# Gate and up projections of 16 experts in Strassen's scheme on 32-column tiles (fp32, one core)

## The reference

```python
cap = EC_CAPACITY_FACTOR * T // N_EXPERTS            # 128 prompt rows, 32 sample rows
aff = jax.nn.softmax((xt @ w_router).astype(F32), axis=-1)
g, idx = lax.top_k(aff.T, cap)
xe = xt[idx]
he = jax.nn.silu(jnp.einsum('ecd,edf->ecf', xe, w_gate)) * jnp.einsum('ecd,edf->ecf', xe, w_up)
ye = jnp.einsum('ecf,efd->ecd', he, w_down) * g[..., None].astype(h.dtype)
y = jnp.zeros((T, D), h.dtype).at[idx.reshape(-1)].add(ye.reshape(-1, D))
```

## Time and profile before

| | |
|---|---|
| Median of 3 runs | 2678.43 us (2675.58 to 2678.94) |
| Profiled execution | 2674.68 us, span 2672.6 us |
| TensorE busy | 2567.5 us, 96% |
| DVE / ACT / POOL busy | 42% / 18% / 12% |
| Granted TensorE clock, mean | 0.985 |
| Expert part | from about 1823 us to the end |

### The profile page before, as it was taken

One profiled execution on the slowest core, in us unless ns is written; L12 is line 12 of the kernel. 1 busy time (PEld: TensorE's weight loads), 2 busy tenths in 40 slices (PEclk: granted clock), 3 DMA queues, 4 the chain that ended last, 5 costly groups with the idle time before them and its releaser, 6 DMA issues.

```text
span 2672.6 us, 37000 instructions
## 1 busy us (share of the span) xinstructions
PE 2567.5 (96%) x15287; PEld 1810.1 (68%) x15287; DVE 1119.8 (42%) x2013; ACT 489.7 (18%) x1114; POOL 313.2 (12%) x310
## 2 busy tenths in 40 slices
PE   7999899999989999999999999977999999999997
PEld 4554455765667777774466477436899889889886
DVE  5556825266774121133430134374334333433433
ACT  3120000144451111102211022210111111111112
POOL 0120103200000101041210001100110010011001
PEclk9999999999999999999999999997999999999999
DMA  4110202000001001022101300236787778778776
GB/s 160 32 51 0 93 28 59 1 1 16 1 25 47 24 24 48 24 88 86 48 16 52 105 32 1 88 132 242 263 275 270 271 262 287 258 260 275 259 270 252
DMA packets 189947, 315.90 MB, mean 118 GB/s; under 512 B 6122, under 2 KB 69951, under 8 KB 189216
## 3 DMA queue, kind: packets, MB, share of 16 engines
q1 hardware_dynamic: 181952, 292.87, 31.6%
q0 software_dynamic: 7904, 21.76, 3.2%
HBM read 288.40 MB, written 26.21 MB: 118 GB/s over the span
## 4 chain that ended last, share of the span: by engine, by line
PE 90%; DVE 8%; ACT 1%; issue 1%; DMA 0%; SPq 0%; POOL 0%; POOLq 0%; DVEq 0%; ACTq 0%
PE banks L827 46%; PE banks L1158 9%; PE banks L1580 9%; PE banks L1018 5%; PE banks L1331 5%; PE banks L1247 5%; PE banks L1425 3%; PE banks L1038 3%; PE banks L1094 2%; DVE arena L2204 2%; PE banks L843 1%; PE banks L1053 1%; PE banks L1547 1%; DVE arena L2650 1%; DVE arena L2653 0%
## 5 line engine op out<-in xcount | busy, mean ns | idle before, releaser
L827 PE MATMUL banks<-arena 128*128 128x160 f32 (+3 forms) x7030 | 1332.6, 351 | 22.3 <-ACT arena L1691 8.0
L827 PEld LDWEIGHTS banks<-arena 128*128 128x128 f32 x7030 | 1050.8, 191 | 322.1 <-issue 268.6
L682 POOL TENSOR_TENSOR arena<-arena 128x512 f32<-128x512 f32 (+2 forms) x112 | 170.0, 1530 | 1208.8 <-DMA arena<-in_w_br_hyena 566.6
L1158 PE MATMUL banks<-arena 128*128 128x320 f32 x896 | 243.2, 432 | 0.5 <-ACT arena L1803 0.5
L1580 PE MATMUL banks<-arena 128*32 128x256 f32 x4320 | 236.2, 379 | 0.0
L1158 PEld LDWEIGHTS banks<-arena 128*128 128x128 f32 x896 | 169.8, 190 | 70.4 <-ACT arena L1803 1.0
L1580 PEld LDWEIGHTS banks<-arena 128*32 128x32 f32 x4320 | 138.9, 110 | 92.7 <-issue 2.5
L2735 DVE TENSOR_TENSOR arena<-arena,banks 128x160 f32<-128x160 f32 x128 | 41.1, 321 | 356.2 <-ACT arena L1956 324.1
L2745 DVE TENSOR_TENSOR arena<-arena 128x512 f32<-128x512 f32 x240 | 149.4, 684 | 14.3 <-DMA arena<-in_w_exp_down 14.3
L1018 PE MATMUL banks<-arena 128*128 128x512 f32 (+1 forms) x384 | 142.9, 522 | 2.5 <-DVE arena L2244 2.5
L1956 ACT ACTIVATE arena<-banks 128x160 f32<-128x160 f32 x120 | 36.5, 304 | 503.8 <-PE banks L827 503.8
(11 more groups left out here) (269 smaller groups left out, 1851.0 us busy)
## 6 DMA issues: line engine op xcount, KB each, us to landing
arena<-in_w_exp_gate SPq DMA_DIRECT2D x32, 2048.0 KB, 8.2
arena<-in_w_exp_up SPq DMA_DIRECT2D x32, 2048.0 KB, 13.1
arena<-in_w_exp_down SPq DMA_DIRECT2D x32, 2048.0 KB, 17.8
arena<-in_w_in SPq DMA_DIRECT2D x36, 512.0 KB, 4.4
arena<-in_x_prompt SPq DMA_DIRECT2D x8, 1024.0 KB, 8.5
residual_rows<-arena SPq DMA_DIRECT2D x10, 512.0 KB, 2.6
normed_rows<-arena SPq DMA_DIRECT2D x10, 512.0 KB, 2.6
arena<-residual_rows SPq DMA_DIRECT2D x5, 1024.0 KB, 13.6
```

The source lines that it names most:

```text
L682: done.inc(pool.tensor_tensor(out, l, r, op))
L827: last = pe.matmul(out, l, r, start=(n == 0), stop=(n == len(pairs) - 1))
L1158: last = pe.matmul(PS[:, 3 * (g % 2) + bank, 0:GN], l[:, k, :], r[:, k, :], start=(k == 0 and which in (G1, G2, G5)), stop=(k == 3), skip_ ...
```

## The change

Gate and up get the scheme that the down product has. The hidden width is cut in two halves h = 0 and 1. For each, the pair of matrices is (gate half, up half), both 1024x512, as if they were the left and right column halves of one matrix of 1024x1024; the third pair is that of down. So an expert has three stages with 9 units each. Names of sums in a stage: c11a and c11b (gate, first 64 slots on one side), c22a and c22b and c12a and c12b (up), c21a and c21b (gate, second slots), sg and sh (sample gate and hidden), ha and hb (the product silu(gate) times up for 256 columns). The order of units is MID or LATE: in LATE (second half, in the loop) the sample's unit s comes last.

Since slots are now stationary, the hidden values come with slots on partitions (`HR`, `HRQ`) and are turned back into `HE`: `turn_half` (4 transposes) twice, `turn_quarters` (2) once. ACT copies them out of PSUM. ACT also does the scaled slot copies into `XET` that DVE did (16 a pass). The weight sums are 8 for each stage on 1024 elements a partition: two `own_weights` for the stage itself (into `W4`), six `next_weights` for the next stage. The token sums of `XET` for the next expert are POOL's (`token_sums`). For expert 0, POOL makes the first six sums of the first pair as twelve of 128x512, before it gathers. The final rows are loaded after the first half of expert 15, into buffers of its first pair, and most of their squares come after its hidden values. Cut to its core:

```diff
+        MID = ("p1a", "p1b", "p6a", "p6b", "p7a", "p7b", "s", "p4a", "p4b")
+        LATE = ("p1a", "p1b", "p6a", "p6b", "p7a", "p7b", "p4a", "p4b", "s")
 # SP
+            def expert_pairs(e, first, which):
...
+                    if not first and n < 2:
+                        sp.wait_ge(sem["gu_mm"], GU * e + (9 * n - 9))
+                    if not first and n == 2:
+                        sp.wait_ge(sem["dn_mm"], e * DN)
...
+            sp.wait_ge(sem["gu_mm"], GU * (NE - 1) + 9)
             for i in range(NT // 2):
                 sp.dma_start(at(FIN_AT[i], 2, D), acc[2 * i * P:2 * (i + 1) * P, :]...
 # POOL
+            pool.wait_ge(sem["w_in_0"], 32)
+            for out, l, r in ((W1[0], b12, b11), (W2[0], b22, W1[0]), (b12, b12, b22)):
+                mixes.wait()
+                for k in range(4):
+                    half_sum(mixes, out[:, k, :], l[:, k, :], r[:, k, :], ALU.subtract)
...
             with pool.Fori(1, NE - 1) as e:
                 gather(e + 1, False)
+                token_sums(e + 1)
                 scatter(e, False)
 # TensorE
-            def gate_up(e, first):
-                wait("xet_ready", e * 4 + 4)
-                for f in range(FF // P):
...
+            def gate_up(e, h, first, order):
...
+                        elif name == "p4a":
+                            if h == 0:
+                                wait("x_sum", 5 * e + 5)
+                            wait("wt_sum", w_summed(e, h, 2))
+                            wait("gu_sum", summed(e, h, order, "c22a"))
+                            unit("gu_mm", (6, False, a22, W4, a_cols), (3, False, XS4, b22, a_cols))
...
+                unit("gu_mm", (7, True, a11, b11, b_cols), (7, True, a12, b21, b_cols))
+                if h == 1:
+                    wait("gu_sum", summed(e, 0, MID, "hb"))
+                    turn_half(0)
...
+            def expert(e, first):
+                gate_up(e, 0, first, MID)
+                gate_up(e, 1, first, LATE)
+                wait("gu_sum", summed(e, 1, LATE, "hb"))
+                turn_half(1)
+                turn_slots(e + 1, False)
+                down(e)
 # turn_slots: the quarter blocks use bank 1, in which the turned half lay
+                if not first:
+                    wait("he_ready", e * 4 - 2)
 # ACT
+                snapshot(e, 1, LATE, 5, "p7b")
+                second_silu(e, 1, LATE, 0)
+                second_silu(e, 1, LATE, 1)
+                snapshot(e, 1, LATE, 6, "s")
+                half_turned(e, 1, 2)
+                sample_silu(e, 1, LATE)
+                slot_blocks(e + 1, 0)
+                rows_down(e, first)
 # DVE
+            def weight_sum(out, l, r, k):
+                ks = slice(2 * k, 2 * k + 2)
+                dve.tensor_tensor(out[:, ks, :], l[:, ks, :], r[:, ks, :], ALU.subtract).then_inc(sem["wt_sum"], 1)
...
+            def second_half(e):
+                gate_first(e, 1, LATE, 0)
+                own_weights(e, 1, 0)
+                gate_first(e, 1, LATE, 1)
+                own_weights(e, 1, 1)
+                next_weights(e, 1, 1, 0)
+                next_weights(e, 1, 1, 1)
+                next_weights(e, 1, 2, 0)
+                up_second(e, 1, LATE, 0)
+                next_weights(e, 1, 2, 1)
+                up_second(e, 1, LATE, 1)
+                next_weights(e, 1, 3, 0)
+                up_first(e, 1, LATE, 0)
+                rows_hidden(e, 1, LATE, 0)
+                next_weights(e, 1, 3, 1)
+                up_first(e, 1, LATE, 1)
+                rows_hidden(e, 1, LATE, 1)
+                sample_gate(e, 1, LATE)
+                sample_hidden(e, 1, LATE)
```

More of the change, by code:

```diff
@@ L1542, in turn_slots @@
                 wait("gather_s", e * 16 + 16)
+                for half, bank in ((0, 0), (1, 2)):
+                    for k in range(4 * half, 4 * half + 4):
+                        last = pe.transpose(PS[:, bank, (k % 4) * P:(k % 4 + 1) * P], XE[:, tiles[k]], ident[:, :])
+                    last.then_inc(sem["xe_tr"], 1)
                 if not first:
[L1544 to L1548, removed]
+                    wait("he_ready", e * 4 - 2)
@@ L1549, in turn_slots @@
                 for c in range(2):
-                    last = pe.transpose(PS[:, 5, c * P:(c + 1) * P], XEQ[:, tiles[c]], ident[:, :])
+                    last = pe.transpose(PS[:, 1, c * P:(c + 1) * P], XEQ[:, tiles[c]], ident[:, :])
                 last.then_inc(sem["xe_tr"], 1)
-            def gate_up(e, first):
-                wait("xet_ready", e * 4 + 4)
-                for f in range(FF // P):
[L1556 to L1564, removed]
@@ new lines, in second_half_begun, with rows_down, copied @@
+            def second_half_begun(e, order):
+                snapshot(e, 1, order, 0, "p1a")
+                first_silu(e, 1, order, 0)
+                snapshot(e, 1, order, 1, "p1b")
+                half_turned(e, 0, 1)
+                first_silu(e, 1, order, 1)
+                snapshot(e, 1, order, 2, "p6a")
+                snapshot(e, 1, order, 3, "p6b")
+                snapshot(e, 1, order, 4, "p7a")
+            def rows_down(e, first):
+                def copied(n, name):
+                    rows, side = (upper, lower) if n < 6 else (lower, upper)
+                    gate = gnow[upper, 2:3] if n == 6 else gnow[lower, 0:1] if n >= 4 else gnow[lower, 1:2]
+                    act.wait_ge(sem["dn_mm"], e * DN + (MID.index(name) + 1))
+                    act.activation(KEPT7[n][rows, :], PS[side, 6 + (n % 2 if n < 6 else 0), 0:256], ACT.Copy, scale=gate
+                                   ).then_inc(sem["dn_kept"], 1)
@@ new lines, in added, with gate_first, up_second @@
+            def added(e, h, order, name, dst, src, n, rows):
+                dve.wait_ge(sem["gu_kept"], kept(e, h, n + 1))
+                dve.tensor_tensor(dst, src, KEPT7[n][rows, :], ALU.add).then_inc(sem["gu_sum"], 1)
+            def gate_first(e, h, order, n):
+                dve.wait_ge(sem["gu_mm"], unit_done(e, h, order, ("p1a", "p1b")[n]))
+                added(e, h, order, "c11", GP[upper, n, :], PS[upper, 6 + n, 0:256], n, upper)
+            def up_second(e, h, order, n):
+                added(e, h, order, "c22", UP[lower, n, :], PS[upper, 3 + n, 0:256], 4 + n, upper)
@@ L2766, in results @@
-            def results(e, first):
-                lower, upper = slice(0, CP // 2), slice(CP // 2, CP)
-                def added(dst, bank, rows, gate, n):
-                    dve.wait_ge(sem["dn_kept"], e * DKEPTS + (n + 1))
-                    dve.scalar_tensor_tensor(dst, PS[rows, bank, 0:256], gate, DKEPT[n][rows, :], ALU.mult, ALU.add
-                                             ).then_inc(sem["y_out"], 1)
+                for n, col in enumerate((gates[:, 0, bass.ds(e, 1)], gswap[:, bass.ds(e, 1)], gates[:, 1, bass.ds(e, 1)])):
+                    dve.tensor_copy(gnow[:, n:n + 1], col).then_inc(sem["gates_now"], 1)
```

528 lines of the change are left out of this document (365 added, 163 removed).

## The result

The changed kernel is slower. It takes 2786.62 us (median of four runs, 2784.56 to 2789.08); the kernel before, on the same chip, takes 2678.68 (four runs, 2675.58 to 2682.19). The ratio is 1.041, with a 95% interval of 1.039 to 1.042. The forecast was 2653.6, with a range to 2675: wrong in sign and by 133 us.

What follows compares the result with a forecast made beforehand. TensorE's own work was taken as the bound. Passes -28.6, expert 0 +0.7, selection +0.5 and end +2.6 made -24.8 from 2674.7: 2649.9, plus 3.7 for the median: 2653.6 us, range 2643 to 2675.

Steps and rivals of the forecast that it cites:

- TensorE's own work: TensorE in the loop: 27 units of 1.727 us plus turnings and changes make 49.3, pass 49.7 instead of 51.74.
- the chain without cover: End of the second half: last product, turnings and ACT's emptying of bank 1 leave TensorE waiting 0.3 to 0.5 us a pass.
- Whether DVE keeps up: DVE in the loop: 24 weight sums of 1.15 us and the rest make 39.8 of 49.7; adds ready when TensorE wants them.
- Rival (a): DVE becomes the bound, from 1.33 us a weight sum; 2711 us at 1.5. Chances 0.09 past 1.42, 0.08 between 1.33 and 1.42.
- (b): Lost cover adds up: flag restarts of 0.1 to 0.2 us and POOL's sums give pass 51.0, 2672 us; chance 0.10.
- POOL's token sums: Five POOL operations a pass during down: 3.4 us, DVE losing up to that, mostly covered by room; taken as 0.
- Before the experts and in expert 0: POOL's twelve first-pair sums, 16 us, beside DVE's selection: +0.5 us; second pair's late load in expert 0: +0.7 us.
- rival (c): POOL's twelve sums push the selection before the experts by 5 to 16 us: 2658 to 2669 us; chance 0.10.
- After the experts: Last expert: seven squares follow ACT's copy, delaying the root; DVE's chain ends at 57.9 us against 55.2, taken as +2.6.
- What the change takes from TensorE: Gate and up in the loop: 128 products, 34.8 us, become 18 units of 1.727, 31.1 us: 3.7 less a pass.
- What it adds on TensorE: Per pass: turning hidden values back 1.2 us, changes between kinds of product 0.3, and an uncovered wait of 0.3 to 0.5.
- Rival (d): Products on 32-column tiles don't keep their pitch, or the granted clock falls; slower; chance 0.02.

Runs made afterwards that it cites:

- written-out: The changed kernel with TensorE's loop over experts 1 to 14 written out as straight code, nothing else: 2652.61 us, ratio 0.991 to the kernel before.
- hinted one: The changed kernel with `hint_back_edge` on TensorE's loop, adding one branch prefetch instruction to the body, head not moved: 2656.47 us, ratio 0.992 to the kernel before.
- split root: The changed kernel with TensorE's loop written out and the final rows' root, reciprocals and scalings done in two parts of five tiles: 2646.86 us, ratio 0.989.
- aligned kernel: The changed kernel with the head of TensorE's loop moved to the start of a block of 256 instructions: 2712.33 us, ratio 1.013 to the kernel before.
- kernel before with the long body: The kernel before with two experts instead of one in the body of TensorE's loop, 7 passes and 6 jumps back: 2700.40 us, ratio 1.009.

## Why the prediction was wrong

**TensorE's own work.** Right. The pass was forecast at 49.7 and is 49.8 wherever no jump disturbs it: the first pass of the changed kernel and all passes of the written-out and the hinted one. In part that is luck, since two small misses cancel in it: 544 MATMULs in 29.56 are 17 units of 1.739, not 1.727, which makes 0.3 more for 27 units, and the chain without cover, put in at 0.3 to 0.5, costs nothing in the loop (below).

**Whether DVE keeps up.** Right. A weight sum's median in the written-out kernel is 1.226 us, and four in a row start 1.13 apart (W was 1.15). DVE is busy for 43.3 of 49.8 in a pass, 87%, where near 85% was forecast. The weight sums of the written-out kernel (min/median/max ns, first and last start), and then TensorE's waits in its experts on what DVE makes:
```profile
L2964 DVE TENSOR_TENSOR arena<-arena x370: 1206/1226/1752, 1833.8 to 2600.4; 128x1024 f32<-128x1024 f32 x185
```
```profile
PE banks L1631 <- DVE arena L2943: 1.9, 1, 1.9
PE banks L1631 <- DVE arena L2990: 1.2, 1, 1.2
PE banks L1614 <- DVE arena L3007: 1.2, 2, 0.7
```
All are single or double events in experts 0 and 15; none returns in each pass, so c22a, c22b and y were there when wanted. Rival (a) is out, and so is (b): the pass is not 51.0, and the turnings' wait, for which 0.3 to 0.5 a pass was put in, is 1.2 in all.

**POOL's token sums.** Too small: 3.4 forecast, 5.6 measured. POOL and DVE in time in the written-out kernel, with the idle time that precedes:
```profile
2072.21 1.03 POOL L811 TENSOR_TENSOR arena<-arena 128x256 f32<-128x256 f32 x1 [27.44 <-ACT arena L2124]
2073.32 0.73 POOL L813 TENSOR_TENSOR arena<-arena 128x256 f32<-128x256 f32 x1
2074.01 0.73 POOL L814 TENSOR_TENSOR arena<-arena 128x256 f32<-128x256 f32 x1
2074.70 1.44 POOL L815 TENSOR_TENSOR arena<-arena 128x128 f32<-128x128 f32 x1
2076.10 1.71 POOL L817 TENSOR_TENSOR arena<-arena 128x256 f32<-128x256 f32 x1
```
```profile
2074.16 3.06 DVE L2964 TENSOR_TENSOR arena<-arena 128x1024 f32<-128x1024 f32 x2 [0.74 <-PE banks L1631]
```
POOL's sum of 128 elements beside DVE takes 1.44, longer than one of 256 (0.73), and DVE's two sums take 3.06 where two cost 2.4. Each delays the other, as the sum of the earlier trace rows had shown. The step's figure was too small by 2.2 us, but what it put down as room did hide it: TensorE waits for none of it in the pass.

**Before the experts and in expert 0.** Right. The selection's wait grew from 12.97 to 13.5, the 0.5 forecast, and rival (c) did not come about. POOL's twelve sums took 15.4 us (16 forecast), from 1770.79 in the changed kernel, and DVE's MAX8 beside them took 0.68, as the mean of the kernel before (678 ns): no measurable slowing, nor of FIND_INDEX8 and MATCH_REPLACE8. Expert 0, from its first turning (1824.95) to the first product of expert 1 (1883.5), takes 58.6 in the written-out kernel against 57.9, for a forecast of +0.7.

**After the experts.** Right: in the written-out kernel the last expert starts at 2580.4 and DVE's chain ends at 2638.3, 57.9 later, the forecast number. The split root shows that the stated cause is the right one.

**The sum** with its four terms gave 2653.6; the written-out kernel, which does the same work, takes 2652.61. That they agree so closely is partly luck. The sum added 3.7 us for the distance of the median from the profiled execution, as it was before; here that distance is 0.6, and the profiled execution itself took 2651.97, 2.1 above the 2649.9 forecast. The passes alone (49.8, not 49.7) make 1.4 of it. For the same reason the 110.4 against 110.2 above is closer than the forecast's terms are known.

**The step that failed** is the one that isn't there. In "What the change takes from TensorE" and "What it adds on TensorE" each instruction was priced by its duration, and the sum took for granted that the next one is always at hand. The next one was not at hand behind 13 jumps: 7.3 us of waiting and some 3 of half clock each, 135 us in all, for a term that the sum doesn't have. The changed pass has 884 MATMULs in place of 554, each with its LDWEIGHTS. Nothing in the prediction counts them as instructions, though the trace of before gave the means: TensorE's instructions in a pass, 1142, and q8 with 12 packets from 1820 on but none from 1930 to 2605, from which one reads that the body is held. That the store has an end, and where, no row of before shows; but a body that grows by 60% was a resource to be bounded from both sides, as the text did for POOL. Rival (d), at a chance of 0.02, was that the products on 32-column tiles don't keep their pitch or that the granted clock falls; it did fall, to 0.50, yet as a consequence, behind each wait, and it accounts for 3 of 10.4 us a pass. As a cause it is refuted by the written-out kernel, which has the same products at full clock. The range reached to 2675 because each of its cases moved single microseconds in a pass; none held a cost that appears whole at a threshold.

## What to carry to other kernels

A change that multiplies the instructions in an engine's loop needs a term for the code: count the engine's instructions in the body, in blocks of 256 from where the head stands, and on TensorE keep them within seven, the most that was held here without a hint (1785 instructions with the head moved, 20 packets from 1820 on; each 32-bit product is four instructions in the trace), or write the loop out (2652.6 us here), or add the hint (2656.5). In a profile this cost shows as waits with "issue" as releaser, once or twice at the same place of each pass but not in the first, and as instruction packets that come in step with the passes. A gain of 2 us a pass can be real, as it was here, and be buried under a threshold that it steps over.

## What was unexpected of the hardware

- For a block of some 256 instructions that TensorE jumped to and didn't hold it waited 2.3 to 3.2 us; for the block behind it, beside weight loads that hold 97% of the DMA engines, 4.4 to 5.5. The place of the loop's head decided whether there were two such waits or one: 2787 against 2712 us.
- The changed body of 1817 instructions is held with the hint (20 packets from 1820 on) and refetched whole without it (137, nine a jump): one block too many costs all of them, not one.
- Two waits with some 7.3 us in all brought the granted clock from 1.00 to 0.50 in every pass, which cost some 3 us; one wait of 2.8 to 3.2 did so behind all 13 jumps of the aligned kernel, for 1.7 us, but waits of 2.8 to 2.9 only behind two of six jumps of the kernel before with the long body.
